# The first unit of each stage issued in the order in which its operand halves appear, a fourth pair of split buffers, and three units held back at each output

## The reference

```python
for l in range(2):                        # first block, l = 0: hybrid mixer, l = 1: retention
    h = rms_norm(x) * (1 + sc_m) + sh_m   # sc, sh, gt: rows of c_act @ ada_w
    x = x + gt_m * mixer(h)               # its last step is a product with w_out
    h = rms_norm(x) * (1 + sc_f) + sh_f
    x = x + gt_f * swiglu(h)              # width 2816
for l in range(2):                        # second block
    h = x @ w_in + b_in                   # recurrence, block attention of three kinds
    x = layer_norm(ALPHA * x + mix @ w_out)
    x = layer_norm(ALPHA * x + peer(x))   # 8 heads pick 16 of 16384 experts for each token
```

## Time and profile before

| | us |
|---|---|
| median of three runs | 2823.83 |
| lowest and highest | 2821.84, 2824.97 |
| span of the profiled execution, first to last instruction | 2822.7 |
| PE busy in it | 2742.5 |
| DVE, ACT busy | 2206.9, 1603.1 |

### The profile page before, as it was taken

One profiled execution on the slowest core, in us unless ns is written; L12 is line 12 of the kernel. 1 busy time (PEld: TensorE's weight loads), 2 busy tenths in 40 slices (PEclk: granted clock), 3 DMA queues, 4 the chain that ended last, 5 costly groups with the idle time before them and its releaser, 6 DMA issues.

```text
span 2822.7 us, 45174 instructions
## 1 busy us (share of the span) xinstructions
PE 2742.5 (97%) x16984; PEld 2418.7 (86%) x16984; DVE 2206.9 (78%) x3851; ACT 1603.1 (57%) x2775; POOL 88.7 (3%) x154
## 2 busy tenths in 40 slices
PE   8998999999999999999999999999999999999998
PEld 5776887977888979999998888888899999988886
DVE  4766888886665668999887888867799989788887
ACT  3433554344554744778894555546457789755553
POOL 1000101010002000000000000020000000000000
PEclk9999999999999999999999999999999999999999
DMA  8433777774556335666668777752466666687775
GB/s 296 155 112 127 263 254 250 248 248 154 189 187 231 114 122 186 214 212 200 201 195 265 242 241 241 236 197 91 151 204 215 204 206 194 216 262 242 241 242 165
DMA packets 211288, 579.69 MB, mean 205 GB/s; under 512 B 24096, under 2 KB 87872, under 8 KB 210048
## 3 DMA queue, kind: packets, MB, share of 16 engines
q1 hardware_dynamic: 161568, 491.00, 53.7%
q0 software_dynamic: 13792, 53.28, 5.6%
q10 hardware_dynamic: 35712, 32.52, 3.3%
HBM read 541.05 MB, written 35.65 MB: 204 GB/s over the span
## 4 chain that ended last, share of the span: by engine, by line
PE 83%; DVE 11%; ACT 3%; issue 1%; DMA 0%; ACTq 0%; DVEq 0%; POOLq 0%
PE psum L762 83%; DVE gmem L2167 3%; DVE wr L2167 2%; ACT gmem L1551 1%; DVE gmem L2170 1%; DVE xmem L2170 1%; ACT wr L1551 1%; ACT crf L1551 1%; DVE xr L2167 1%; DVE oh_r L2170 0%; DVE xmem L2167 0%; DVE small L2949 0%; DVE wr L2170 0%; PE psum L840 0%; DVE gmem L3063 0%
## 5 line engine op out<-in xcount | busy, mean ns | idle before, releaser
L2167 DVE TENSOR_TENSOR wr<-raw,wr 128x1024 fp32r<-128x1024 f32 (+1 forms) x814 | 995.6, 1224 | 406.1 <-ACT wr L1551 401.1
L762 PE MATMUL psum<-xr,wr 128*128 128x256 f32 (+1 forms) x9760 | 1287.9, 292 | 16.6 <-DVE xr L2167 9.3
L762 PEld LDWEIGHTS psum<-xr,wr 128*128 128x128 f32 x9760 | 1231.9, 191 | 59.5 <-DVE xr L2167 14.7
L1551 ACT ACTIVATE wr<-raw 128x1024 fp32r<-128x1024 f32 x808 | 847.8, 1050 | 276.8 <-PE psum L762 256.2
L762 PE MATMUL psum<-wr,cr 128*128 128x512 f32 x3072 | 697.4, 389 | 5.0 <-DVE cr L2167 5.0
L762 PEld LDWEIGHTS psum<-wr,cr 128*128 128x128 f32 x3072 | 576.3, 188 | 125.7 <-ACT cr L1551 3.3
L1551 ACT ACTIVATE cr<-xmem 128x256 fp32r<-128x256 f32 x256 | 107.2, 419 | 339.0 <-PE psum L762 336.9
L1551 ACT ACTIVATE gmem<-psum 128x512 f32<-128x512 f32 (+2 forms) x303 | 169.0, 570 | 204.1 <-PE psum L762 187.8
L762 PE MATMUL psum<-wr,xr 128*128 128x512 f32 (+1 forms) x960 | 231.2, 393 | 8.1 <-DVE wr L2170 2.7
L762 PEld LDWEIGHTS psum<-wr,xr 128*128 128x128 f32 x960 | 172.7, 189 | 50.8 <-issue 6.7
L2170 DVE SCALAR_TENSOR_TENSOR oh_r<-cst,keep,keep_r 128x256 fp32r<-128x256 f32 x512 | 213.2, 479 | 0.0
(11 more groups left out here) (174 smaller groups left out, 1532.9 us busy)
## 6 DMA issues: line engine op xcount, KB each, us to landing
raw<-in_uv SPq DMA_DIRECT2D x512, 512.0 KB, 4.9
raw<-in_ffn_in SPq DMA_DIRECT2D x88, 512.0 KB, 3.7
gs<-xmem ACTq DMA_DIRECT2D x248, 128.0 KB, 3.7
xmem<-gs SPq DMA_DIRECT2D x248, 128.0 KB, 4.4
gmem<-in_ada_w POOLq DMA_DIRECT2D x56, 512.0 KB, 5.0
raw<-in_ffn_out SPq DMA_DIRECT2D x44, 512.0 KB, 4.0
raw<-in_ada_w SPq DMA_DIRECT2D x40, 512.0 KB, 4.1
raw<-in_ret_a SPq DMA_DIRECT2D x32, 512.0 KB, 4.5
```

Of the source, the lines that this page charges most:

```text
L762: ins = pe.matmul(o, a, b, start=first and i == 0, stop=final and i == len(pairs) - 1, skip_group_check=skip)
L1551: return act.activation(o, a, func, **k)
L2167: return dve.tensor_tensor(o, a, b, op)
```

## The change

`NSPLIT` becomes 4, and from the hybrid mixer's output on (`NEAR`) ACT and DVE split three units ahead instead of two; ACT's split waits for unit j - 4. The 8 KB on each partition for the fourth pair come from the area for software DMAs, which is set to 8192.

At a stage head PE no longer waits for the last lo. The head leaves a tag in `fresh`, and the first unit is issued by `early_unit` (or the `fresh` branch of `out_unit`, `early_half`, the `e == 0` branch of `peer_v`): first all products with the activation's hi, the k of g = 0 and then of g = 1, each behind the wait for ACT's copy, then the products with its lo. The groups of dummy matmuls behind the second token half are dropped. In a layer norm the second token half of x is made in two column halves, so four DVE operations in place of two, and the first of its transposes waits for the first half only (`x half`). In `ada_norm` the product of x and the scale row for token half 0 moves from the norm into the residual; ACT writes its squares elsewhere for that.

`out_last` holds three units back (hybrid, FFN, retention, `peer_v`); ACT and DVE split nothing more behind the unit that follows the stage's last, and split the next two at the end of the norm (`split(0)`, new on ACT). At the mixers' outputs of the second block two are still held, beside the first two units that are used in halves; `nsa_turn` of half 0 uses bank 0 instead of 2. `peer_v` has three buffers for c (the third in `keep_r`), weighs three blocks ahead, halves two ahead, and waits for each c only where `out_last` first uses it.

```diff
-NSPLIT = 3
+NSPLIT = 4
...
     HYB_OUT = (4, 5, 6, 7, 0, 1, 2, 3)
+    NEAR = len(units)
     units += [(dr["hyb_out"][k], UNIT) for k in HYB_OUT]
     ffn_out = [dr["ffn_out"][l].rearrange("(k p) n -> k p n", p=P) for l in range(2)]
...
             self.unit += step
-            while self.next <= min(self.unit + 2, NU - 1):
+            far = 2 if self.unit < NEAR else NSPLIT - 1
+            while self.next <= min(self.unit + far, NU - 1):
                 self.next += 1
                 if self.next - 1 not in plain | added:
...
     ccr = cr.rearrange("p (i s t) -> p i s t", i=2, s=2)
+    third = keepr[:, 0:512].rearrange("p (s t) -> p s t", s=2)
+    c_at = [ccr[:, 0], ccr[:, 1], third]
     gabs = cr[:, 0:128].rearrange("p (s k n) -> p s k n", s=2, k=KD)
...
+
         def col_unit(o, src):
             j, hi, lo = next_unit()
             hi, lo = (v.rearrange("p (k n) -> p k n", k=KD) for v in (hi, lo))
+            if fresh:
+                early_unit(hi, lo, src, o, o).then_inc(*W.pe.up(j))
+                return
             mm3(o, [(hi[:, k, :], lo[:, k, :], src[:, 0, k, :], src[:, 1, k, :])
                     for k in range(KD)]).then_inc(*W.pe.up(j))
+
+        def early_unit(hi, lo, src, o, o_low):
+
+            tag = fresh.pop()
+            for g in range(2):
+                pe.wait_ge(*N.act[tag, "hi", 1, g])
+                for k in range(4 * g, 4 * g + 4):
+                    mm(o, [(hi[:, k, :], src[:, 0, k, :]), (lo[:, k, :], src[:, 0, k, :])], k == 0, False, True)
+            for g in range(2):
+                pe.wait_ge(*N.dve[tag, "lo", 1, g])
+                ins = mm(o_low, [(hi[:, k, :], src[:, 1, k, :]) for k in range(4 * g, 4 * g + 4)], False, g == 1, True)
+            return ins
...
+            if fresh:
+                early_unit(hi, lo, src, both_[:, 0, :], both_[:, 1, :]).then_inc(*W.pe.up(j))
+                return
...
+            if fresh:
+                tag = fresh.pop()
+                for a in range(2):
...
-        def out_last(b, c_of, ks, sig):
+        def out_last(b, c_of, ks, sig, ready=None):
 
...
                     for k, (j, hi, lo) in zip(ks, held):
+                        if ready and (a, n) == (0, 0):
+                            ready(k)
                         ch, cl = c_of(k)
                         ins = mm3(bank(b + 2 * a + n), [(ch[:, quarter(a)], cl[:, quarter(a)], hi[:, e], lo[:, e])],
-                                  False, k == ks[1], True)
+                                  False, k == ks[-1], True)
...
             if g:
-                pe.wait_ge(*N.dve["hyb", "lo", 1, 1])
+                fresh.append("hyb")
...
-                busy(3, 1)
-            pe.wait_ge(*N.dve[tag, "lo", 1, 1])
+                if a == 0:
+                    busy(3, 1)
+            fresh.append(tag)
...
-            pe.wait_ge(*N.dve["hyo", "lo", 1, g])
+            fresh.append("hyo")
...
-            if k not in (2, 3):
+            if k not in (1, 2, 3):
                 out_unit(0, xr, k, 4, 4)
-            elif k == 2:
-                out_last(0, rows_of(xr), (2, 3), "hyb out")
+            elif k == 1:
+                out_last(0, rows_of(xr), (1, 2, 3), "hyb out")
...
+            if k < FM - 3:
                 out_unit(4, hid, k, 0, FM)
-            elif k == FM - 2:
-                out_last(4, rows_of(hid), (FM - 2, FM - 1), ("ffn out", l))
+            elif k == FM - 3:
+                out_last(4, rows_of(hid), (FM - 3, FM - 2, FM - 1), ("ffn out", l))
...
         def nsa_turn(l, a):
-            b = 2 + a
+            b = 3 * a
...
+        def early_half(l, a, units_):
+
+            pe.wait_ge(*N.act[("on", l), "hi", a, 1])
+            for k, j, hi, lo in units_:
+                for n in range(2):
+                    e = slice(512 * n, 512 * n + 512)
+                    c = xr[:, 0, k, quarter(a)]
+                    mm(bank(2 + 2 * a + n), [(c, hi[:, e]), (c, lo[:, e])], k == 4, False, True)
+            pe.wait_ge(*N.dve[("on", l), "lo", a, 1])
...
             if k == 4:
                 first_half(l, 1, first_two[1:2])
                 claim(2, 3)
-                pe.wait_ge(*N.dve[("on", l), "lo", 0, 1])
-                first_half(l, 0, first_two)
+                early_half(l, 0, first_two)
...
                 for a in range(2):
-                    pe.wait_ge(*N.dve[tag, "x", a])
                     for g_n in range(2):
+                        pe.wait_ge(*N.dve[tag, "x half" if (a, g_n) == (1, 0) else "x", a])
                         b = 4 + 2 * a + g_n
                         claim(b)
                         turn4(b, x[:, a, :], 512 * g_n, N.pe.up((tag, "t", a, g_n)))
                         drained[b] = N.dve[tag, "lo", a, g_n]
-                    busy(1, 1)
+                    if a == 0:
+                        busy(1, 1)
...
+            c = c_at[e % 3]
+            if e == NEXP - 3:
+                out_last(0, lambda k: (c_at[k % 3][:, 0, :], c_at[k % 3][:, 1, :]), (NEXP - 3, NEXP - 2, NEXP - 1), ("l2", l),
+                         lambda k: pe.wait_ge(*X.dve["c", l, k]))
+            if e >= NEXP - 3:
+                return
+            j, hi, lo = next_unit()
+            if e == 0:
+                pe.wait_ge(*X.act["c", l, 0])
...
+                        v = slice(n * 512, (n + 1) * 512)
+                        mm(bank(2 * a + n), [(ccr[:, 0, 0, quarter(a)], hi[:, v]), (ccr[:, 0, 0, quarter(a)], lo[:, v])],
+                           True, False, True)
+                pe.wait_ge(*X.dve["c", l, 0])
+                for a in range(2):
...
+            split(0)
...
         def hybrid_out(k):
-            split()
+            if k in (2, 3):
+                ahead.step()
+            else:
...
         def halve(l, e):
             act.wait_ge(*X.dve["w", l, e])
-            if e >= 2:
-                act.wait_ge(*W.pe[base_v[l] + e - 2])
-            f(ccr[:, e % 2, 0, :], gel[e % 8], AF.Copy).then_inc(*X.act.up(("c", l, e)))
+            if e >= 3:
+                act.wait_ge(*W.pe[base_v[l] + e - 3])
+            f(c_at[e % 3][:, 0, :], gel[e % 8], AF.Copy).then_inc(*X.act.up(("c", l, e)))
 
         def peer_v(l, e):
-            if e + 1 < NEXP:
-                halve(l, e + 1)
-            split()
+            if e + 2 < NEXP:
+                halve(l, e + 2)
+                split()
+            else:
+                ahead.step()
...
-                tt(h[:, a, :], x[:, a, :], aa, ALU.mult).then_inc(*N.dve.up())
+                if a:
+                    tt(h[:, a, :], x[:, a, :], aa, ALU.mult).then_inc(*N.dve.up())
...
+                if a == 0 and tag:
+                    if A.dve.value:
+                        dve.wait_ge(*A.dve.now)
+                    own(X)
+                    tt(norms[tag][0][:, 0, :], x[:, 0, :], norms[tag][2], ALU.mult).then_inc(*N.dve.up())
...
             if k == 3:
-                residual("hyb out", top(0), hy_tmp)
+                residual("hyb out", top(0), hy_tmp, ("ffn", 0))
+            elif k == 2:
+                ahead.step()
...
+                for h in range(1 + a):
+                    e = slice(512 * h, 512 * h + 512) if a else slice(0, D)
+                    stt(x[:, a, e], src[:, a, e], mv[:, 2 * a:2 * a + 1], g[:, e], ALU.subtract,
+                        ALU.mult).then_inc(*N.dve.up())
+                    own(N)
+                    stt(x[:, a, e], x[:, a, e], mv[:, 2 * a + 1:2 * a + 2], b_[:, e], ALU.mult,
+                        ALU.add).then_inc(*N.dve.up((tag, "x half" if h < a else "x", a)))
...
         def peer_v(l, e):
+            if e + 3 < NEXP:
+                weigh(l, e + 3)
             if e + 2 < NEXP:
-                weigh(l, e + 2)
-            if e + 1 < NEXP:
-                halve(l, e + 1)
+                halve(l, e + 2)
                 split()
+            elif e + 1 < NEXP:
+                ahead.step()
...
-    nc = _bacc.Bacc("TRN2", target_bir_lowering=False, num_devices=1)
+    nc = _bacc.Bacc("TRN2", target_bir_lowering=False, num_devices=1, dynamic_dma_scratch_size=8192)
```

More of the change, by code:

```diff
@@ L812, in out_unit @@
             j, hi, lo = next_unit()
+            if fresh:
+                tag = fresh.pop()
+                for a in range(2):
+                    pe.wait_ge(*N.act[tag, "hi", a, k // 4])
+                    for n in range(2):
+                        e = slice(512 * n, 512 * n + 512)
+                        mm(bank(b + 2 * a + n), [(src[:, 0, k, quarter(a)], hi[:, e]), (src[:, 0, k, quarter(a)], lo[:, e])],
+                           k == k0, False, True)
+                for a in range(2):
+                    pe.wait_ge(*N.dve[tag, "lo", a, k // 4])
+                    for n in range(2):
+                        e = slice(512 * n, 512 * n + 512)
+                        ins = mm(bank(b + 2 * a + n), [(src[:, 1, k, quarter(a)], hi[:, e])], False, k == of - 1, True)
+                ins.then_inc(*W.pe.up(j))
+                return
             for a in range(2):
@@ L1238, in ret_out_ @@
```

(53 more changed lines are left out.)

56 lines of the change are left out of this document (29 added, 27 removed).

## The result

The changed kernel takes 2791.4 us (median of 4 runs, 2788.9 to 2792.5) against 2824.4 of the kernel before on the same chip: 0.988 of it, 95% interval 0.9866 to 0.9894. The forecast was 2794, and the range 2786 to 2811 holds the time. The profiled execution spans 2789.3 us instead of 2822.7, 33.4 less, against 30.0 forecast.

A forecast was written before the change was run, and what follows sets the result against it. PE was taken as the bound, busy 2742.5 of 2822.7 us. Stage ends 3.2, heads 14.7, waits 10.5 and clock 1.6 sum to 30.0: span 2792.7, plus 1.1 gives 2793.8, said as 2794; range 2786 to 2811.

The forecast's parts named there:

- Stage ends: Three `ada_norm`s and `mix_start`: with three units held DVE ends the residual one bank behind PE; 0.8 us each, 3.2 us.
- Stage heads: At stage heads PE starts the first real unit earlier, without waiting for the last lo; together 14.7 us.
- some 1.2: Hybrid output's last four units: a new wait of some 1.2 us, as `out_last` asks for the fourth at once.
- the 0 of the forecast: At `NEAR` two splits follow each other directly; could lose 1.2 us or win as much, taken as 0.
- the first norm's 2.3: At the first norm PE could start at 42.75 instead of 45.15: 2.3 us gained.
- The waits: PE waits that the fourth pair and third c take away, in `mix_out`, `peer_v` and for split units: together 10.5 us.
- The split-unit waits of the routing: Of 8.0 us of PE waits for split units, mostly in the routing, half go: 4.0 us, bounds 0 and 8.0.
- Clock: Behind the longest wait, 2.81 us, the clock is 0.50; with the wait cut it stays at 2.4 GHz: 1.6 us.
- The second unit late: Rival, 17%: at the heads the second unit's split ends no earlier, 13 us of gains vanish, 2807.
- The clock at the heads: Rival, 6%: six heads losing their last dummies go on at the slow level, 1.6 us each, about 2804.
- The gain swallowed: Rival, 8%: the lead ends behind the first norm and in the attention; 5 us or less remain, 2819 to 2829.
- POOL's loads: Rival, 7%: the smaller software-DMA area makes POOL's loads slow, in `ffn_out` and retention 87 us, about 2881.

The follow-up runs named there:

- the order undone: Changed kernel, but PE again waits for the last lo and runs plain first units at every head, second half's dummies back: 2806.8 us, ratio 0.9956.
- The kernel with the switch moved: Changed kernel with held units asked for one at a time, plus the switch to three ahead moved into the first FFN: 2791.5 us, ratio 0.9886.
- the depth alone: Kernel before plus only the fourth pair, splits three ahead from the first FFN on, and the smaller software-DMA area: 2815.8 us, ratio 0.9982.
- the depth and the third c: Kernel before plus the fourth pair, splits three ahead, smaller software-DMA area and third c buffer, halves made one unit earlier: 2809.7 us, ratio 0.9955.
- the 11 us: Changed kernel with splits three units ahead from the first unit on: 2803.2 us, ratio 0.9922, 11.4 us more than the changed kernel beside it.

## Why the prediction was right, point by point

**Stage ends**, 3.2 us. The mechanism holds and the size was a little high. From the first dummy to the first unit the kernel before takes 10.44, 10.03 and 10.44 us at the three `ada_norm`s, and the kernel with three held units and the order undone 9.71 at each; at `mix_start` it is 4.80 us from the first transposes against 4.06. That is 0.7, 0.3, 0.7 and 0.7, together 2.5. Taking the third unit out of the changed kernel shows other parts: 1.2 to 1.3 at each `ada_norm`, nothing at `mix_start`; why they differ stays open. The moved multiplication is free: DVE waits 0.63 us for PE ahead of bank two and still ends one bank behind.

**Stage heads**, 14.7 us. The first units start within 0.15 us of the last transposes, as forecast. At the `ada_norm`s the second unit waits 0.35 and 0.25 us and then not at all, the forecast's order. `mix_start`'s, with the stage end ahead of it, is 2.4 us against 2.45. The new wait at the hybrid output is 1.24 against "some 1.2". At the switch to three ahead PE waits 0.86 us. The kernel with the switch moved gains 1.2 us on its neighbour there and has lost 1.3 again by the end of the hybrid output, so the 0 of the forecast holds. At `peer_q`'s heads the first unit gains 1.9 us and the lead settles 1.5 and 1.6 higher, against 1.65 forecast; the third layer norm keeps 1.8. Wrong: the first norm's 2.3. PE does start early, at 44.62, but the lead over `qkv` is 0.2 us, and with the order undone nothing is lost. ACT waits there for raw loads (3.6, 3.1, 1.9 and 1.0 us), which an earlier PE does not move.

**The waits**, 10.5 us. `mix_out` gives 2.0 in each layer, as forecast. `peer_v` gives 0.75 between its first and last product against 1.03, since its held units wait 0.32 and 0.54 for a split. The split-unit waits of the routing are the term that was sized most wrongly: "I take half, 4.0, since a late DVE can appear again at the next product". It does not, and the whole is larger than the listed 8.0: the lead grows by 4.6 and 4.7 us, 9.3 in all, outside the bounds of 0 and 8.0. They took the list for the whole. Of the routing it shows 3.7 us a layer, in seven waits for a split unit and one for ACT, but a wait costs more than it lists. In the kernel before:

```profile
1041.73 6.00 PE L762 MATMUL psum<-xr,wr 128*128 128x256 f32 x48
1047.57 1.06 PE L762 MATMUL psum<-gmem 128*128 128x128 f32 x8
...
1117.78 8.90 PE L762 MATMUL psum<-xr,wr 128*128 128x256 f32 x72 [0.48 <-ACT xmem L1551]
1127.36 8.86 PE L762 MATMUL psum<-xr,wr 128*128 128x256 f32 x72 [0.68 <-DVE wr L2167]
```

Without a wait, 48 matmuls take 5.84 us from start to start, so 72 take 8.76. The 72 in front of the wait take 9.58, which is 0.82 more where 0.68 is listed. The list counts from the end of the last matmul as the profile draws it, 0.28 us behind its start, and the next could have started after 0.12. Eight waits a layer are thus worth 3.7 + 8 x 0.16 = 5.0 us, and the new wait of 0.66 takes some 0.8 back. Some 0.4 us a layer stay unexplained.

**Clock**, 1.6 us. This step failed. The row behind the head reads

```profile
46.00:48.00 2.00, 2.00 (x19) 2.00 (x18) 2.00 (x3) 0.00 (x0) 1.47 (x3) 1.00 1.22 271
```

as forecast, but the cause given is not shown. The kernel with the order undone has the same 2.81 us wait there, and behind it the full clock:

```profile
45.50 6.74 PE L766 MATMUL psum<-xr,wr 128*128 128x256 f32 x54 [2.81 <-DVE xr L2255]
...
46.00:48.00 2.00, 2.00 (x20) 2.00 (x19) 0.57 (x1) 0.53 (x1) 0.00 (x0) 1.00 0.87 155
```

Of the four kernels with this wait two fall to the slow level behind it (the kernel before, the depth alone) and two do not (the order undone, the depth and the third c). Nor was the stretch worth 1.6 us. The lead rises through it from 0.5 us to 1.9 (49.58 against 47.71), and at 69.78 against 69.98 it is gone, in the stretch in which ACT waits for raw loads. And the total was not lowered: ahead of the last stage each profile has three slow stretches, 5.1 us lost in both, from 46.5, 176.2 and 985.2 us on in the kernel before and from 17.9, 1905.5 and 1926.0 on in the changed one. Over all fast executions the mean clock is 0.997 for either kernel. The last two stretches of the changed kernel lie in the second attention:

```profile
1904.00:1908.00 4.00, 4.00 (x22) 3.61 (x22) 2.38 (x5) 3.00 (x7) 0.00 (x0) 0.69 0.36 131
...
1924.00:1928.00 4.00, 4.00 (x29) 3.90 (x29) 2.89 (x14) 2.87 (x10) 0.00 (x0) 0.75 0.35 131
```

This is where the lead fell from 27.5 to 24.1. Those of the kernel before at 176.2 and 985.2 us had given it 1.6 and 1.5, so clock is worth -0.3 us in these two profiles, against 1.6 forecast.

**Not in the prediction**: 2.3 us of pace in the second FFN (next section but one). The rest agrees: 30.0, plus 5.3 for the routing and 2.3 for the pace, less 2.1 at the first norm, 1.9 of clock and 0.2 over all other terms, is 33.4. That 2794 was within 3 us of the time is in part luck of signs: 7.6 us too little stand against 4.0 too much.

**The rivals.** The second unit late: its wait is 0.35, so no. The clock at the heads: 1.00 in the windows behind all six. The gain swallowed: true of the first stage alone. POOL's loads: 4.9 us.

## What to carry to other kernels

In a program written out engine by engine, a queue's depth is first of all a place in the order. A split that stands one unit earlier pays where PE is the bound and DVE's work comes in bursts, probably costs where PE waits for DVE's chains (that reading of the 11 us is not shown), and moves the bound to the next thing that DVE makes just in time (here c). So change depth by stage, and look for the next late operand at once. If an end holds n units back, see that the next stage's first unit still has a pair and a place for its split, and ask for the held units one at a time. When a wait list is used as a bound, add to each wait what its last matmul is drawn too long (0.16 us here for 256 columns), and compare starts of the same instruction across the stretch. Take them from the engine that bounds: ScalarE's first activation behind `peer_q`'s head had a lead 0.5 us smaller than TensorE's, for it stood behind a wait for a load that TensorE did not feel.

## What the hardware showed that was not expected

The slow clock level comes and goes at other places in two executions of one kernel. The changed kernel's second profile has, where the first has 1.00 throughout:

```profile
952.00:956.00 4.00, 4.00 (x22) 3.73 (x21) 2.12 (x4) 2.53 (x4) 0.00 (x0) 0.64 0.08 20
...
972.00:976.00 4.00, 4.00 (x17) 3.63 (x16) 3.58 (x14) 2.20 (x6) 0.00 (x0) 0.58 0.31 114
```

Over the 13 profiles the clock lost ahead of the last stage is 1.7 to 12.0 us, in steps of about 1.7, nearly all of it in the first 250 us and in the attention stages, where PE waits often. So a single profile can't carry a clock term of 1.6 us. The Trainium skill ("TensorE: Matmul & The Clock Gate", "What's actually happening") says of the warm-up at a kernel's start that its point varies from run to run of one kernel. What the two profiles show is more than it states: stretches in the midst of the kernel that come in one execution and not in the other.

The wide units of `ffn_in` (a product of 512 columns, then one of 256) run at one of two paces for a whole stage. In the timeline, of the kernel before and then of the changed one, whose first unit has 8 matmuls more:

```profile
702.14 124.64 PE L762 MATMUL psum<-xr,wr 128*128 128x512 f32 x704 [0.88 <-DVE xr L2167]
826.62 3.57 PE L762 MATMUL psum<-wr,hid_r 128*128 128x512 f32 x15
```

```profile
692.95 122.36 PE L766 MATMUL psum<-xr,wr 128*128 128x256 f32 x712
815.15 7.23 PE L766 MATMUL psum<-wr,hid_r 128*128 128x512 f32 x31
```

Start to start, a pair takes 353 ns in the one and 347 in the other, granted clock 1.00 in both; 2.3 us over the stage. In the second FFN the slow pace is seen in the kernel before and in the one with the order undone, and the fast one in the eleven other profiles, those of the depth alone on the kernel before among them; in the first FFN a kernel may run at either pace for some 30 us, and all end at the fast one. What sets it stays open.
